# Up projection on unnormalised rows: the inverse root applied when the accumulators are evicted

## The chip, the cores and the metric

The kernel runs on one core of a Trainium2 chip. The metric is the device time of one execution in microseconds (us); the kernel before has a median of 2216.98 us over three runs (2213.57 to 2222.62).

## The reference, cut to what matters

One layer of a trunk is computed for 384 tokens (128 of a prompt, 256 of a sample), all in float32. The part around the change is the end of the mixer and the start of the feed-forward block:

```python
    x = x + g1 * y                      # y = mixer output @ w_out, D = 2048
    h2 = rmsnorm(x, lp['n2']) * (1.0 + sc2) + sh2
    x = x + g2 * conv_ffn(h2, lp['w_up'], lp['ffn_conv_w'], lp['ffn_conv_b'], lp['w_down'])

def conv_ffn(h, w_up, dw_w, dw_b, w_down):
    u, gv = jnp.split(h @ w_up, 2, axis=-1)      # 2 x 5632 columns
    u = depthwise_conv(u, dw_w, dw_b)            # 3 taps along the tokens
    return (jax.nn.silu(u) * gv) @ w_down
```

`rmsnorm` divides each token's row by the root of its mean square. The scales and shifts `sc2`, `sh2` belong to a channel and to the prompt or the sample.

## The kernel before, in words

**Split products.** Every large matmul is done in the reduced-precision float32 type three times: each operand is split into a high part and a low part, and high times high, high times low and low times high are added up in the same accumulator (`three`, lines 760 to 764). A weight part of 128x1024 is split by ScalarE (`hi`, line 1293) and VectorE (`lo`, line 1622); four such parts are held at a time, so `hi(n)` waits until TensorE has used part n-4. Parts are numbered through all stages. The `w_out` stage has parts P_OUT to P_OUT+31, eight to each of four blocks of 512 output columns; the `w_up` stage has P_UP to P_UP+175, four to each of 44 blocks of 256 columns (22 pairs: a block of `u`, then its block of `gv`). I write part P_UP+4 as "up part 4", and so on.

**Weights from memory.** SyncE alone issues the weight loads (line 501), 1 MB each, which is two parts, into a ring of four pieces. A load waits until the piece it overwrites has been split. In the first pair of the up stage something stands between the loads:

```python
            for i in range(DFF // BLK):
                load_block(P_UP + 2 * PARTS * i, a["w_up"][0], BLK * i, BLK)
                if i == 0:
                    sp.wait_ge(s_oc, 3 * N_OUT)
                    sp.dma_start(X_dram.rearrange("t p c -> p t c"), x2).then_inc(s_xs, 16)
                load_block(P_UP + 2 * PARTS * i + PARTS, a["w_up"][0], DFF + BLK * i, BLK)
```

So the loads of up parts 4 to 7 are issued after the residual of the last output block is finished (`s_oc` is 12) and after the store of `x2` (3 MB) to `x_mid`.

**The output projection.** TensorE runs the blocks j = 0 to 3 (`out_part`). VectorE adds each block, gated, to `x2` (`residual`, lines 2006 and 2007: six operations of 128x512). ScalarE squares it with a running sum (`squares`, line 1498).

**The transition.** When all four blocks are in `x2`, VectorE reduces the squares, GpSimd raises to the power -1/2 (line 652), VectorE scales `x2` by the root (line 2030), TensorE transposes it (`turn2`, lines 1213 and 1220: 48 transposes of 128x128), ScalarE and VectorE apply scale and shift (lines 1517 and 2036), and ScalarE and VectorE split the result (lines 1523 and 2041) into `h_split`, high and low, 16 rows of 384 words each (one for each 128 channels). `h_split` held the output projection's moving data before. Half of the transposes are placed ahead of the first up part and the rest behind up parts 0 and 1.

**The up projection.** The weights are stationary, 128x128; 384 columns of `h_split` stream past them. It has 22 x 2 x 2 x 16 x 3 = 4224 matmuls. Each pair's `u` accumulators are copied by ScalarE to `up2` (lines 1543, 1544), convolved by VectorE (2076 to 2078), passed through SiLU by ScalarE (1554) and multiplied with `gv` from its accumulators by VectorE (2086, 2087) into `act`. The down projection then splits `act` (lines 1564 and 2111) as its stationary operand.

Engines run their instructions strictly in the program's order. The printed functions below stand as they are in the kernel before.

Of the kernel before, what the change touches and what calls it, by code (L numbers as in the profile page):

```python
# [29 lines left out]
CHUNK = 64  # L30
DFF = 11 * D // 4
# [3 lines left out]
BT = 4  # L35
# [187 lines left out]
def build(nc, a, out):  # L223
    ctx = ExitStack()
    with ctx:
# [31 lines left out]
        NA = 52900 - C_END - 4 * P - 2 * KT - 192 - 2 * KT - 64 - 11 - RING * PIECE - 2 * SPLITS * PART - 2 * KT * TOK - 2400  # L257
# [5 lines left out]
        with ExitStack() as early:  # L263
            wsp = sb("w_split", 2 * SPLITS * PART, F32R, early)
            hsp = sb("h_split", 2 * KT * TOK, F32R, early)
            asp = sb("a_split", 2400, F32R, early)
        wmix = sb("w_mix", 2 * SPLITS * PART)
        hf = sb("h_f32", 2 * KT * TOK)
        ubuf = sb("u_buf", 2400)
        hh = hsp[:, 0:KT * TOK].rearrange("p (k n) -> p k n", k=KT)  # L270
        hl = hsp[:, KT * TOK:].rearrange("p (k n) -> p k n", k=KT)
# [42 lines left out]
        assert o <= 2400  # L314
# [47 lines left out]
        late = [(ubuf, HW * i) for i in range(2400 // HW)]  # L362
# [16 lines left out]
        xn2, o = carve(arena, o, 3, D)  # L379
        assert o <= NA  # L380
        ytmp, _ = carve(ubuf, 0, 2, OUT_W)
        mtmp, o = carve(ubuf, 0, 4, TOK)
        ssq2, o = carve(ubuf, o, 3, N_OUT)
        assert o <= 2400
# [7 lines left out]
        assert o <= 2400  # L392
# [14 lines left out]
        s_const, s_x, s_vrow, s_lnrow = sem("s_const"), sem("s_x"), sem("s_vrow"), sem("s_lnrow")  # L407
# [13 lines left out]
        s_rpl, s_rdp = sem("s_rpl"), sem("s_rdp")  # L421
# [22 lines left out]
        s_ssq2, s_xn2, s_xtp, s_xts, s_h2 = sem("s_ssq2"), sem("s_xn2"), sem("s_xtp"), sem("s_xts"), sem("s_h2")  # L444
# [24 lines left out]
        def used(eng, n):  # L469

            if n < P_DOWN:
                eng.wait_ge(s_blk, DONE.get(n, n + 1))
            else:
                eng.wait_ge(s_kd, n - P_DOWN + 1)

# [281 lines left out]
        def _(pe):  # L757
# [445 lines left out]

            for j in range(N_OUT):
                for p in range(0 if j else 3, OUT_PARTS):
                    out_part(j, p)

            def turn2(q):
                pe.wait_ge(s_xn2, q + 1)
                if q >= 2:  # L1210
                    pe.wait_ge(s_hmp, 4 * (q - 1))
                for k in range(4 * q, 4 * q + 4):
                    last = tr(ps[:, 6 + q % 2, toks(k % 4)], xn2[:, 0, toks(k)], ident)
                last.then_inc(s_xtp, 1)
                for j in range(2):
                    if q:
                        pe.wait_ge(s_hms, 4 * (q - 1) + 2 * j + 2)
                    for k in range(2):
                        for t in range(2):
                            last = tr(ps[:, 4 + j, P * (2 * k + t):P * (2 * k + t + 1)], xn2[:, 1 + t, toks(4 * q + 2 * j + k)], ident)  # L1220
                    last.then_inc(s_xts, 1)

            pe.wait_ge(s_oc, 3 * N_OUT)
            turn2(0)
            turn2(1)
            for i in range(DFF // BLK):
                for w in range(2):
                    if i >= 2:
                        pe.wait_ge(s_uc if w == 0 else s_uact, 2 * (i - 1))
                    for p in range(PARTS):  # L1230
                        n = P_UP + PARTS * (2 * i + w) + p
                        pe.wait_ge(s_lo, rank(n) + 1)
                        if i == 0 and w == 0:
                            pe.wait_ge(s_h2, KQ * (p + 1))
                        w_hi, w_lo = parts(n, KQ)
                        for s in range(2):
                            for k in range(KQ):
                                q = KQ * p + k
                                last = three(ps[:, 4 * (i % 2) + 2 * w + s, 0:TOK], w_hi[:, k, toks(s)], w_lo[:, k, toks(s)],
                                             hh[:, q, :], hl[:, q, :], start=(q == 0), stop=(q == KT - 1))  # L1240
# [37 lines left out]
        def _(ac):  # L1278
# [216 lines left out]
            def squares(j):  # L1495
                ac.wait_ge(s_oc, 3 * (j + 1))
                for t in range(3):
                    AC(xn2[:, t, OUT_W * j:OUT_W * j + OUT_W], x2[:, t, OUT_W * j:OUT_W * j + OUT_W], ACT.Square, accum_out=ssq2[:, t, j:j + 1]).then_inc(s_ssq2, 1)

            for n in range(P_OUT, P_UP):  # L1500
                if n >= P_OUT + 2 * OUT_PARTS and (n - P_OUT) % OUT_PARTS == OUT_PARTS // 2:
                    squares((n - P_OUT) // OUT_PARTS - 2)
                if n == P_OUT + 3:
                    ac.wait_ge(s_fy, 3 * GROUPS)
                if n > P_OUT + 2:
                    hi(n)
# [6 lines left out]
            def mod_p(k):  # L1513
                ac.wait_ge(s_xtp, k // 4 + 1)
                if k >= 4:
                    ac.wait_ge(s_h2, k - 3)
                AC(mtmp[:, k % 4, 0:P], ps[:, 6 + k // 4 % 2, toks(k % 4)], ACT.Identity, scale=scol[:, k, 0:1],
                   bias=modcol[:, 3 * KT + k, 0:1]).then_inc(s_hmp, 1)

            def h2_hi(k):  # L1520
                ac.wait_ge(s_hms, k + 1)
                ac.wait_ge(s_hmp, k + 1)
                AC(hh[:, k, :], mtmp[:, k % 4], ACT.Copy).then_inc(s_hh2, 1)

            for k in range(KT + 1):
                if k < KT:
                    mod_p(k)
                if k:
                    h2_hi(k - 1)
# [674 lines left out]
```

## Time and profile before

| what | value |
|---|---|
| median of 3 runs | 2216.98 us (2213.57 to 2222.62) |
| the profiled execution | 2212.79 us, of which the trace spans 2211.0 us |
| TensorE busy | 2078.0 us, 94% of the span |
| VectorE busy | 1058.3 us, 48% |
| ScalarE busy | 746.3 us, 34% |
| granted TensorE clock, mean | 0.978 of full speed |
| mean memory traffic | 155 GB/s |

All times below count from the start of the trace's span. "Busy" of TensorE is modelled for its pipelined matmuls, so where matmuls follow each other the distance from start to start is the cost of one. The output projection ends near 1068 us, the up projection near 1826 us.

### The profile page before, as it was taken

Reading aid. Unit: us, or ns where it says so; the run is one execution under the profiler, and the core shown is the slowest. Engines: PE = TensorE matmul, PEld = TensorE weight load, DVE = VectorE, ACT = ScalarE, POOL = GpSimd, SP = SyncE. Lnnn points to the kernel's source line nnn. Section 1 sums busy time; section 2 is a strip of 40 time slices with the busy share of each in tenths; the row PEclk is TensorE's granted clock in tenths of the full one; section 3 lists DMA queues with packets and bytes.
Section 4 is the critical chain, followed back from the end, with each engine's and each line's share of the span. In section 5 each row is a group of like instructions: output and inputs, shape, how many; then the busy total and the mean of one; then the engine's idle time right before and its main releaser. Section 6 shows DMA issues by size and latency. Waiting matters only on the chain.

```text
span 2211.0 us, 43887 instructions
## 1 busy us (share of the span) xinstructions
PE 2078.0 (94%) x19367; PEld 1818.5 (82%) x19367; DVE 1058.3 (48%) x1833; ACT 746.3 (34%) x1230; POOL 154.7 (7%) x248
## 2 busy tenths in 40 slices
PE   4899999999878888899799999999999999999997
PEld 2688888777557777788699999999999998887886
DVE  1432225555557777653644444444444444445444
ACT  2331222222455444423433223323323333333433
POOL 1000000000324434200000000000000000000000
PEclk8899999999899999999899999999999999999999
DMA  9888778776410010173343343343343436443341
GB/s 387 323 280 293 284 251 285 264 280 215 104 31 9 11 23 13 61 266 115 133 134 125 123 134 121 127 133 118 130 133 116 133 128 234 133 131 101 131 133 58
DMA packets 195999, 343.01 MB, mean 155 GB/s; under 512 B 14253, under 2 KB 137827, under 8 KB 193696
## 3 DMA queue, kind: packets, MB, share of 16 engines
q1 hardware_dynamic: 194416, 335.14, 44.4%
q0 software_dynamic: 1392, 5.05, 0.8%
q8 instruction: 153, 2.51, 0.5%
q14 instruction: 38, 0.31, 0.0%
HBM read 332.62 MB, written 10.31 MB: 155 GB/s over the span
## 4 chain that ended last, share of the span: by engine, by line
PE 85%; DVE 8%; DMA 2%; issue 2%; ACT 2%; POOL 1%; DVEq 0%; POOLq 0%; ACTq 0%
PE ps L762 25%; PE ps L764 24%; PE ps L763 24%; PE ps L796 4%; DMA ring<-in_w_mod_dram 1%; PE ps L1118 1%; PE ps L993 1%; PE ps L1001 1%; PE ps L995 1%; POOL w_mix L652 0%; PE ps L1011 0%; DVE h_split L1684 0%; PE ps L944 0%; PE ps L928 0%; PE ps L914 0%
## 5 line engine op out<-in xcount | busy, mean ns | idle before, releaser
L1622 DVE TENSOR_TENSOR w_split<-ring,w_split 128x1024 fp32r<-128x1024 f32 (+1 forms) x392 | 475.3, 1219 | 724.9 <-ACT w_split L1293 724.4
L1293 ACT ACTIVATE w_split<-ring 128x1024 fp32r<-128x1024 f32 (+1 forms) x392 | 406.8, 1051 | 827.0 <-PE ps L764 561.3
L762 PE MATMUL ps<-h_split,w_split 128*128 128x384 f32 x1776 | 599.9, 338 | 10.7 <-DVE w_split L1622 6.4
L764 PE MATMUL ps<-h_split,w_split 128*128 128x384 f32 x1776 | 596.5, 336 | 0.0
L763 PE MATMUL ps<-h_split,w_split 128*128 128x384 f32 x1776 | 596.4, 336 | 0.0
L762 PEld LDWEIGHTS ps<-h_split,w_split 128*128 128x128 f32 x1776 | 335.6, 189 | 23.9 <-issue 16.1
L763 PEld LDWEIGHTS ps<-h_split,w_split 128*128 128x128 f32 x1776 | 335.5, 189 | 0.0
L764 PEld LDWEIGHTS ps<-h_split,w_split 128*128 128x128 f32 x1776 | 335.4, 189 | 0.0
L762 PE MATMUL ps<-w_split,h_split 128*128 128x512 f32 (+1 forms) x528 | 199.4, 378 | 1.1 <-DVE w_split L1622 1.1
L763 PE MATMUL ps<-w_split,h_split 128*128 128x512 f32 (+1 forms) x528 | 195.9, 371 | 0.0
L764 PE MATMUL ps<-w_split,h_split 128*128 128x512 f32 (+1 forms) x528 | 195.7, 371 | 0.0
L762 PE MATMUL ps<-w_split,a_split 128*128 128x512 f32 x348 | 136.6, 393 | 6.1 <-DVE h_f L2100 4.8
L764 PE MATMUL ps<-w_split,a_split 128*128 128x512 f32 x348 | 136.5, 392 | 0.0
L763 PE MATMUL ps<-w_split,a_split 128*128 128x512 f32 x348 | 136.2, 391 | 0.0
L762 PEld LDWEIGHTS ps<-w_split,h_split 128*128 128x128 f32 x528 | 99.6, 189 | 29.0 <-issue 8.3
L796 PE MATMUL ps<-ring,c 128*2 128x256 f32 x1536 | 104.6, 406 | 17.2 <-DMA ring<-in_w_mod_dram 14.4
L764 PEld LDWEIGHTS ps<-w_split,h_split 128*128 128x128 f32 x528 | 99.7, 189 | 17.1
L763 PEld LDWEIGHTS ps<-w_split,h_split 128*128 128x128 f32 x528 | 99.7, 189 | 16.1
L652 POOL TENSOR_TENSOR stat<-stat,expb 128x3 f32<-128x3 f32 (+1 forms) x6 | 5.7, 953 | 1297.3 <-DVE stat L2134 1126.7
L796 PEld LDWEIGHTS ps<-ring,c 128*2 128x2 f32 x1536 | 34.2, 87 | 71.0 <-issue 24.0
L762 PEld LDWEIGHTS ps<-w_split,a_split 128*128 128x128 f32 x348 | 65.6, 188 | 21.4 <-DVE h_f L2100 6.0
L1564 ACT ACTIVATE a_split<-arena 128x384 fp32r<-128x384 f32 x58 | 30.4, 526 | 152.9 <-PE ps L764 152.8
(368 smaller groups left out, 2505.5 us busy)
## 6 DMA issues: line engine op xcount, KB each, us to landing
ring<-in_w_mod_dram SPq DMA_DIRECT2D x96, 1024.0 KB, 8.2
ring<-in_w_up_dram SPq DMA_DIRECT2D x88, 1024.0 KB, 5.1
ring<-in_w_in_dram SPq DMA_DIRECT2D x46, 1024.0 KB, 5.6
ring<-in_w_down_dram SPq DMA_DIRECT2D x44, 1024.0 KB, 5.3
ring<-in_w_out_dram SPq DMA_DIRECT2D x16, 1024.0 KB, 5.6
arena<-in_x_sample_dram SPq DMA_DIRECT2D x4, 1024.0 KB, 15.0
x_mid<-arena SPq DMA_DIRECT2D x1, 3072.0 KB, 10.2
h_f<-x_mid SPq DMA_DIRECT2D x1, 3072.0 KB, 10.2
```

The lines of the kernel that those rows point to most:

```text
L652: nc.gpsimd.tensor_tensor(ap, ap, minus_half.broadcast_to(list(ap.shape)), ALU.pow).then_inc(done, 1)
L762: mm(o_, lh, rh, start=start, stop=False)
L763: mm(o_, lh, rl, start=False, stop=False)
L764: return mm(o_, ll, rh, start=False, stop=stop)
L796: last = mm(ps[32 * g:32 * g + 2, i % 2, 0:BLK], c2_t[:, 2 * q:2 * q + 2], w_raw[:, g, :], start=(q == 0), stop=(q == KT - 1))
L993: mm(ps[half(hp), 4 * z + c, at], Nm[z][half(c), h, :], TTm[z][half(c), h, :], start=True, stop=True)
L995: last = mm(ps[half(hp), 4 * z + c, at], TTm[z][half(c), h, :], ident[half(c), half(c)], start=True, stop=True)
L1001: last = mm(ps[half(c), 4 * z + hp, HD * i:HD * i + HD], XT[z][half(hp), c, 1, HD * i:HD * i + HD], XT[z][half(hp), c, 0, HD * i:HD * i + ...
L1118: last = mm(o_, bkT[z][half(hp), q, i, c], zrT[z][half(hp), i, :, c], start=True, stop=True)
L1293: AC(wh[k % SPLITS][:, 0:width(n)], arrived(n), ACT.Copy).then_inc(s_hi, 1)
L1564: AC(ah[i % 3], act[:, i % FT, :], ACT.Copy).then_inc(s_ah, 1)
L1622: V.tensor_tensor(wl[k % SPLITS][:, 0:w], arrived(n), wh[k % SPLITS][:, 0:w].bitcast(F32), ALU.subtract).then_inc(s_lo, 1)
```

## The change

- **No normalisation ahead of the transposes.** `x2` itself is transposed. The inverse root of each token is applied when the up accumulators are evicted: VectorE multiplies two accumulators at a time (`up_raw`, `act_raw`) with a row of roots `rrow`. That row is made by three small matmuls of a constant with diagonal matrices of the roots (`root_row`), placed behind up part 4.
- **The shift as two more columns.** `sh2` must not be multiplied by the root, so it is streamed as two extra columns of the moving operand (prompt and sample). Every up matmul has 386 columns (`UPC`), and the rows of the split operand are 388 words apart (`UPS`). The product of the shift is added at eviction, as a bias on ScalarE and in a combined operation on VectorE.
- **Transposes and splits inside the last output blocks.** `turn2(k)` now does one block of 128 channels (three transposes); k = 0 to 11 are placed ahead of the last two parts of output blocks 1 to 3. The splits `h2_hi` and `h2_lo` of k = 0 to 11 are placed among weight parts 30 to 34 (`H2_AT`), each waiting until the output projection has used what it overwrites (`y_free`). k = 12 to 15 need the last block's residual; their transposes stand in the middle of up part 2, and their scaling and splitting stand behind the splits of up parts 4 and 5 on both engines.
- **Squares spread.** `squares(2)` and `squares(3)` stand behind the splits of up parts 3 and 5; each square now waits for the one before it. The residuals of blocks 0 to 2 are placed earlier among the weight splits.
- SyncE's program is not changed.

```diff
+UPC = TOK + 2
+UPS = TOK + 4
...
             for j in range(N_OUT):
                 for p in range(0 if j else 3, OUT_PARTS):
+                    if j and p >= OUT_PARTS - 2:
+                        turn2(4 * (j - 1) + 2 * (p - OUT_PARTS + 2))
+                        turn2(4 * (j - 1) + 2 * (p - OUT_PARTS + 2) + 1)
                     out_part(j, p)
...
-                        if i == 0 and w == 0:
-                            pe.wait_ge(s_h2, KQ * (p + 1))
...
+                                if i == w == s == 0:
+                                    pe.wait_ge(s_h2, 9 if q < 8 else 14 if q < 12 else h2_count(q))
+                                last = three(ps[:, 4 * (i % 2) + 2 * w + s, 0:UPC], w_hi[:, k, toks(s)], w_lo[:, k, toks(s)],
+                                             h2h[:, q, 0:UPC], h2l[:, q, 0:UPC], start=(q == 0), stop=(q == KT - 1))
+                            if (i, w, p, s) == (0, 0, 2, 0):
+                                for k in range(12, KT):
+                                    turn2(k)
                         last.then_inc(s_blk, 1)
-                        if i == 0 and w == 0 and p < 2:
-                            turn2(p + 2)
+                        if (i, w, p) == (0, 1, 0):
+                            root_row()
...
+            shift_hi(1)
             squares(N_OUT - 2)
-            for p in range(PARTS):
-                hi(P_UP + p)
+            hi(P_UP + PARTS)
+            hi(P_UP + PARTS + 1)
             squares(N_OUT - 1)
+            scale_even(12)
+            h2_hi(12)
+            scale_even(14)
+            for k in range(13, KT):
+                h2_hi(k)
...
+            shift_lo(1)
             residual(N_OUT - 1)
+            lo(P_UP + PARTS)
+            lo(P_UP + PARTS + 1)
+            scale_odd(13)
+            h2_lo(12)
+            scale_odd(15)
+            for k in range(13, KT):
+                h2_lo(k)
 
             dv.wait_ge(s_ssq2, 3 * N_OUT)
...
+                    V.tensor_copy(shift_up, ps[:, b_:b_ + 2, TOK:UPC])
+                    V.tensor_tensor(up_raw, ps[:, b_:b_ + 2, 0:TOK], rrow.unsqueeze(1).to_broadcast([P, 2, TOK]), ALU.mult).then_inc(s_uraw, 1)
...
+                    V.tensor_copy(shift_act, ps[:, b_:b_ + 2, TOK:UPC])
+                    link(V.tensor_tensor(act_raw, ps[:, b_:b_ + 2, 0:TOK], rrow.unsqueeze(1).to_broadcast([P, 2, TOK]), ALU.mult))
```

## Rows read from the trace of the kernel before

**Rows 1.** Windows: length, busy time of PE, PEld, DVE, ACT, POOL (records), granted clock, DMA share, GB/s.
```profile
1068.50:1086.80 18.30, 4.92 (x25) 4.44 (x25) 15.15 (x31) 7.76 (x19) 0.85 (x1) 0.67 0.73 258
...
1088.00:1090.00 2.00, 2.00 (x8) 2.00 (x7) 1.76 (x4) 0.66 (x2) 0.00 (x0) 0.50 1.10 350
...
1200.00:1300.00 100.00, 100.00 (x578) 100.00 (x578) 42.29 (x55) 30.61 (x42) 0.00 (x0) 1.00 0.39 127
```

**Rows 2.** Timeline, all engines, end of the output projection to the first up matmul.
```profile
1068.18 0.39 PE L764 MATMUL ps<-w_split,h_split 128*128 128x512 f32 x1
1068.61 0.69 DVE L2006 TENSOR_TENSOR u_buf<-ps,arena 128x512 f32<-128x512 f32 x1 [1.41 <-PE ps L764]
1068.67 1.06 ACT L1293 ACTIVATE w_split<-ring 128x1024 fp32r<-128x1024 f32 x1 [2.73 <-PE ps L764]
...
1072.96 0.63 ACT L1498 ACTIVATE arena<-arena 128x512 f32<-128x512 f32 x1 [3.24 <-DVE arena L2007]
1072.97 1.22 DVE L1622 TENSOR_TENSOR w_split<-ring,w_split 128x1024 fp32r<-128x1024 f32 x1
...
1074.94 0.17 DVE L2024 TENSOR_REDUCE stat<-u_buf 128x3 f32<-128x12 f32 x1 [0.75 <-ACT arena L1498]
...
1086.80 0.66 PE L762 MATMUL ps<-h_split,w_split 128*128 128x384 f32 x1 [2.13 <-DVE h_split L2041]
```

**Rows 3.** Timeline of TensorE, first up parts.
```profile
1091.72 0.34 PE L762 MATMUL ps<-h_split,w_split 128*128 128x384 f32 x1
...
1093.29 0.60 PE L1213 MATMUL ps<-consts,arena 128*128 128x128 f32 x4
1093.72 1.04 PE L1220 MATMUL ps<-consts,arena 128*128 128x128 f32 x8
...
1102.13 0.41 PE L762 MATMUL ps<-h_split,w_split 128*128 128x384 f32 x1 [0.83 <-DVE h_split L2041]
```

**Rows 4.** Issues of the DMA view, windows at 1030 and 1073 us: KB, us to landing.
```profile
ring<-in_w_up_dram SPq DMA_DIRECT2D x1, 1024.0 KB, 5.2
...
x_mid<-arena SPq DMA_DIRECT2D x1, 3072.0 KB, 10.2
ring<-in_w_up_dram SPq DMA_DIRECT2D x1, 1024.0 KB, 13.8
```

**Rows 5.** Timeline, then waits, of SyncE's queue, 1000 to 1140 us.
```profile
1030.22 8.53 SPq L501 DMA_DIRECT2D ring<-in_w_up_dram  x2
1072.96 0.37 SPq L606 DMA_DIRECT2D x_mid<-arena  x1
1073.37 65.11 SPq L501 DMA_DIRECT2D ring<-in_w_up_dram  x9
...
SPq L606 <- DVE arena L2007: 34.2, 1, 34.2
```

**Rows 6.** Timeline of ScalarE after the splits of `h_split`.
```profile
1105.12 2.94 ACT L1293 ACTIVATE w_split<-ring 128x1024 fp32r<-128x1024 f32 x3
...
1111.93 0.38 ACT L1544 ACTIVATE u_buf<-ps 128x256 f32<-128x256 f32 x1
```

**Rows 7.** Timeline of TensorE at other widths of the moving operand.
```profile
1055.04 0.39 PE L763 MATMUL ps<-w_split,h_split 128*128 128x512 f32 x1
...
1055.72 0.39 PE L763 MATMUL ps<-w_split,h_split 128*128 128x512 f32 x1
...
544.79 0.28 PE L763 MATMUL ps<-w_split,h_split 128*128 128x256 f32 x1
...
545.15 0.28 PE L763 MATMUL ps<-w_split,h_split 128*128 128x256 f32 x1
...
563.00 1.17 PE L873 MATMUL ps<-u_buf,consts 128*128 128x399 f32 x3
564.01 0.82 PE L876 MATMUL ps<-consts,arena 128*128 128x128 f32 x6
```

**Rows 8.** Groups by line and shape, VectorE, 940 to 2211 us: busy us, mean ns.
```profile
L2041 DVE TENSOR_TENSOR h_split<-u_buf,h_split 128x384 fp32r<-128x384 f32 x16 | 8.8, 550 | 0.2 <-ACT h_split L1523 0.2
```

More of the change, by code:

```diff
@@ L361, in build @@
         assert o <= O_RKV, (o, O_RKV)
-        late = [(ubuf, HW * i) for i in range(2400 // HW)]
+        late = [(ubuf, HW * i) for i in range(2368 // HW)]
         late += [(arena, o + HW * i) for i in range((O_RKV - o) // HW)]
@@ L391, in build @@
         sg2, o = carve(ubuf, o, 2, TOK + 1)
-        assert o <= 2400
+        assert o <= 2368
         x3, o = carve(hf, 0, 3, D)
@@ L1202, in _, with turn2, root_row @@
             pe.wait_ge(s_cyh, 1)
+            def turn2(k):
+                pe.wait_ge(s_oc, 3 * (k // 4 + 1))
+                if 2 <= k < 14:
+                    pe.wait_ge(s_hms if k % 2 else s_hmp, k // 2)
+                for t in range(3):
+                    last = tr(ps[:, 6 + k % 2 if k < 14 else k - 10, toks(t)], x2[:, t, toks(k)], ident)
+                last.then_inc(s_xtp, 1)
             for j in range(N_OUT):
                 for p in range(0 if j else 3, OUT_PARTS):
+                    if j and p >= OUT_PARTS - 2:
+                        turn2(4 * (j - 1) + 2 * (p - OUT_PARTS + 2))
+                        turn2(4 * (j - 1) + 2 * (p - OUT_PARTS + 2) + 1)
                     out_part(j, p)
[L1208 to L1225, printed above, removed]
+            def root_row():
+                pe.wait_ge(s_rdiag, 1)
+                for t in range(3):
+                    last = mm(ps[:, 6, toks(t)], consts[:, C_MEAN:C_MEAN + P], rdiag[:, t, :], start=True, stop=True)
+                last.then_inc(s_rrow, 1)
             for i in range(DFF // BLK):
@@ L1497, in squares @@
                 for t in range(3):
[L1498 to L1503, printed above, removed]
-                    ac.wait_ge(s_fy, 3 * GROUPS)
-                if n > P_OUT + 2:
-                    hi(n)
+                    AC(junk_sq, x2[:, t, OUT_W * j:OUT_W * j + OUT_W], ACT.Square, accum_out=ssq2[:, t, j:j + 1]).then_inc(s_ssq2, 1)
@@ new lines, in shift_hi @@
+            def shift_hi(q):
+                ac.wait_ge(s_blk, y_free(8 * q + 7, 0))
+                AC(h2h[:, 8 * q:8 * q + 8, TOK:UPC], modcol[:, 3 * KT + 8 * q:3 * KT + 8 * q + 8, :], ACT.Copy).then_inc(s_hh2, 1)
+            for n in range(P_OUT + 3, P_UP + PARTS):
+                m = n - P_OUT
+                if m >= 2 * OUT_PARTS and m % OUT_PARTS == OUT_PARTS // 2:
+                    squares(m // OUT_PARTS - 2)
+                if m == 3:
+                    ac.wait_ge(s_fy, 3 * GROUPS)
+                if m >= 2 * OUT_PARTS and m % OUT_PARTS in (1, 2):
+                    scale_even(4 * (m // OUT_PARTS - 2) + 2 * (m % OUT_PARTS - 1))
+                hi(n)
+                for k in H2_AT.get(m, ()):
+                    h2_hi(k)
+                if m == OUT_PARTS * N_OUT + 1:
+                    shift_hi(0)
@@ L1520, in h2_hi @@
[L1520 to L1529, printed above, removed]
+            scale_even(12)
+            h2_hi(12)
+            scale_even(14)
+            for k in range(13, KT):
+                h2_hi(k)
             for b in range(2 * (DFF // BLK) + 1):
@@ L1532, in _ @@
                 if b < 2 * (DFF // BLK):
-                    for p in range(PARTS if b else 0):
+                    for p in range(2 if b == 1 else 0, PARTS if b else 0):
                         hi(P_UP + PARTS * b + p)
@@ L1999, in _, with residual @@
             dv.wait_ge(s_fc, 3 * GROUPS)
-            def residual(j):
+            def residual(j, tiles=range(3)):
                 used(dv, P_OUT + OUT_PARTS * (j + 1) - 1)
-                for t in range(3):
+                for t in tiles:
                     n = 3 * j + t
@@ L2061, in _ @@
                 if b < 2 * (DFF // BLK):
-                    for p in range(PARTS if b else 0):
+                    for p in range(2 if b == 1 else 0, PARTS if b else 0):
                         lo(P_UP + PARTS * b + p)
@@ L2084, in _ @@
                         dv.wait_ge(s_usg, f + 1)
[L2085 to L2087 removed]
+                        V.scalar_tensor_tensor(act[:, f, 0:P], act_raw[:, s, 0:P], shift_act[:, s, 0:1], sg2[:, s, 0:P], ALU.add, ALU.mult)
+                        V.scalar_tensor_tensor(act[:, f, P:TOK], act_raw[:, s, P:TOK], shift_act[:, s, 1:2], sg2[:, s, P + 1:TOK + 1], ALU.add, ALU.mult).then_inc(s_uact, 1)
             lo(P_DOWN + SPLITS - 1)
```

150 lines of the change are left out of this document (88 added, 62 removed).

## The prediction

> **What bounds the kernel now.** I read the page first, then windows, then timelines. In the up projection TensorE is without a gap at full clock while VectorE is busy 42% and ScalarE 31% of the time [rows 1]. So there only what TensorE does itself costs time. The place where it idles is the transition: in 18.30 us it works 4.92 us [rows 1], because residual, squares, root, scaling, transposes and splits follow one another [rows 2].
>
> Call T the end of the output projection. The last matmul starts at 1068.18 [rows 2], one lasts 0.227 us from start to start (three in 0.68 us [rows 7]), so T = 1068.41. I count up to the point where no loss follows: up part 2 starts at 1102.13 [rows 3], and from T to there 33.72 us pass. By then 48 of the up matmuls are done, at 173.3 ns each (577 starts to 100 us would be 173.3, the row has 578 [rows 1]), which is 8.32 us. **The transition loses 33.72 - 8.32 = 25.40 us.** This is all that the change can attack, and 0.5% of the time is 11.1 us, about what a measurement of this kernel can tell from no change.
>
> **Transposes and roots on TensorE.** Four transposes take 1093.72 - 1093.29 = 0.43 us [rows 3], 0.108 each. The 36 of k = 0 to 11 go into the output blocks, where TensorE is the bound: 3.9 us. They wait for nothing: their residuals are finished parts earlier, and the splits of weights that run ahead by four parts of 4.1 us give ScalarE and VectorE the room for the scaling. The 12 of k = 12 to 15 cost 1.3 us in up part 2. The three root matmuls are true float32 ones of 128 columns; the nearest row, 399 columns, takes (564.01 - 563.00)/3 = 0.337 us a record [rows 7], so at 128 columns, two records each, between 0.4 us (by columns, the whole being 6 x 0.108 = 0.65) and 2.0 us (6 x 0.337); I take 0.7, as by columns.
>
> **The start of the up projection.** Parts 0 and 1 need k = 0 to 7, whose splits are queued among weight parts 30 to 33 and are done some 5 us ahead of T. k = 8 to 11 stand behind weight part 34, which can be split when part 30 is used, 4.7 us before T. Four high and low splits at 0.55 us [rows 8] end near T + 1, and the shift's splits behind weight part 35 near T + 2.8; both are needed at T + 8.3. So TensorE starts at T, not at T + 18.4 (1086.80), and at full clock.
>
> TensorE then runs 48 matmuls (8.3 us), 12 of part 2 (2.1 us), 12 transposes (1.3 us; their `s_oc` of 12 comes at T + 7.1, below) and 12 more matmuls, and comes to k = 12 in part 3 at **T + 13.8**.
>
> **What k = 12 waits for.** This is the step that decides. On ScalarE `scale_even(12)` stands behind the splits of up parts 4 and 5, on VectorE `scale_odd(13)` and `h2_lo(12)` too. These weights are loaded only after the last residual, behind the 3 MB store; SyncE's program is unchanged. Before, SyncE sat 34.2 us on that wait [rows 5], issued the store at 1072.96 and the load 0.41 us later [rows 5]. That load took 13.8 us to land where an undisturbed one takes 5.2, since the store took 10.2 [rows 4]. It landed at 1087.2, hidden, because ScalarE wanted it only at 1105.12 [rows 6]. The change removes that cover. Step by step from T:
>
> - The high split of part 35 starts 0.26 after T and takes 1.06 [rows 2]; the low split takes 1.22 [rows 2]: T + 2.55. `shift_lo(1)`: 0.2, T + 2.75.
> - The residual's six operations take 1072.96 - 1068.61 = 4.35 [rows 2]: T + 7.1. (Before, it came first, at T + 4.55.)
> - Store issued, load 0.41 later, landed 13.8 after: **T + 21.3**.
> - ScalarE: two splits, 1.06 + 0.98 (three take 2.94 [rows 6]), T + 23.35. `squares(3)`: before 1.98 [rows 2], now each waits for the last; between 2.0 and 2.8, I take 2.4: T + 25.75. Scaling: 0.38 for the wider of its two evictions [rows 6], about 0.55 for both. High split about 0.5, by [rows 8]: T + 26.8.
> - VectorE's low split 0.55 and the semaphores: **T + 27.6**.
>
> TensorE idles 27.6 - 13.8 = **13.8 us**. Queued behind ScalarE's wait are the squares too, so the root comes at about T + 33; `root_row` is wanted after up part 4, at T + 39, so that is covered. k = 13 comes another 0.3 us late, then the rows keep pace.
>
> **The clock.** Before, after the idle transition, TensorE ran at 0.50, its level of 1.2 GHz, until 1091.72 [rows 1, 3]: 15 matmuls in 4.92 us where full clock takes 2.60, a cost of 2.3 us. After 13.8 us of idling I expect the same 2.3.
>
> **Sum of the transition after:** 3.9 + 1.3 + 0.7 + 13.8 + 0.3 + 2.3 = 22.3 us, where 25.4 stood: a gain of 3.1.
>
> **Two more columns.** At full clock 512 columns take 226.7 ns, 384 take 173.3, 256 take 120 (three in 0.36 us) [rows 7, 1]: columns at 2.4 GHz and a fixed 13.3 ns. Two columns add 0.83 ns; times 4224 is 3.5 us, all of it on the bound. No row shows this operand type at a width or a row distance that isn't a multiple of 128 words. From below the cost is 0 (if the fixed part hid it; three widths on one line speak against that). From above: columns counted in sixteens, 400, would be 6.7 ns each, 28.2 us. I take the line, because rows of 399 words read by plain float32 matmuls, starting at any word, take 0.337 us for 2 x 399 columns, which is 332.5 ns and 4 ns more [rows 7]: no rounding and no misalignment shows.
>
> The Trainium skill (SBUF — State Buffer, Specifications) says that SBUF has 16-byte lines and that crossing to a new one is penalised. Rows 388 words apart keep their phase to such lines, and 386 words touch 97 lines where 384 touch 96. By that rule 388 columns' time would be paid, as an estimate 7.0 us in place of 3.5. No run here shows it.
>
> **Evictions.** To a pair of blocks (33.3 us) VectorE gets `up_raw` and `act_raw`, 768 elements each, between 0.69 (512 elements) and 1.22 (1024) [rows 2], about 0.95, and two tiny copies: 2.3 us more, where it idles 19 of 33 us [rows 1]. The weight splits queued behind run three parts ahead, 12.5 us, which hides this and ScalarE's wait for `up_raw`. Cover gone, it would be 22 x 2.3 = 50 us, but it would need VectorE to double. Only the last pair shows: the down projection's second weight operand waits for `act`; 1.3 us more in that chain, most of it behind 4.1 us of matmuls. I take 0.2 (0 to 1.3).
>
> **Total:** -3.1 + 3.5 + 0.2 = **+0.6 us**. Against its own execution, 2212.8 becomes 2213.4; that execution lies 4.2 us under the median. On the median: 2216.98 + 0.6 = 2217.6, say 2218.
>
> **Rivals.**
>
> *The load is not in the way* (faster). Then the transition loses 3.9 + 1.3 + 0.7 and some 1.5 us (0 to 3) for k = 12 to 15, which ScalarE and VectorE could bring at about T + 13 to T + 16: 7.4 us. Gain 18.0, less 3.7: 14.3, so 2203. For it: all else is ready. Against it: the load can't be issued before the residual is done, at T + 7.1, and would have to land at once; even a plain 5.2 us [rows 4] leaves 13.8 - 8.6 = 5.2 us idle, a gain of about 8.0, which is still within 0.5%. Past 0.5% needs 11.7 us off. I may have misread ScalarE's order or the overlap of store and load.
>
> *Matmuls of 386 columns cost more than their columns* (slower). Each ns is 4.2 us. The balance without the width is -2.9, so over 0.5% slower begins at 14.0 us, 3.3 ns each, eight columns' worth. In sixteens: 2217.0 - 2.9 + 28.2 = 2242. Against it speaks the float32 row, for it that this type may be read in another manner.
>
> *Columns in fours* (the rule above, as a mechanism: 388 in place of 386): 1.67 ns x 4224 = 7.0 us, 2217.0 - 2.9 + 7.0 = 2221, no change that can be told.
>
> *The whole does nothing*, as the gap was covered: excluded, since TensorE's idle time is on the chain.
>
> **Chances.** Forecast (stall of 10 to 17 us) 0.68, its own range 2213 to 2223; fours 0.07; load not in the way 0.13; wide matmuls 0.12. Hence faster 0.13, same 0.75, slower 0.12. The range, 2202 to 2227, takes in the faster case and leaves out most of the wide one and some of the tails.
>
> **What the profile after would show.** Up matmuls 174.2 ns apart (574 starts in 100 us, not 578); a first up matmul right behind the output projection; ScalarE waiting for DMA at line 1293 until about 21 us after T, the landing still 13 to 14 us after issue; TensorE idle for some 14 us in the fourth up part, then the low clock for about 15 matmuls. I am wrong if that wait is below 5 us, or if up matmuls stand more than 176 ns apart.

## The result, and the profile after

The changed kernel has a median of **2231.23 us** (2225.86 to 2232.21, five runs), the kernel before 2216.62 us in as many. The ratio is **1.0055**, 95% interval 1.004 to 1.007: slower, by 0.4 to 0.7% (12.2 us by the ratio, 14.6 us by the medians), where +0.6 us was forecast, and outside the range of 2202 to 2227. The profiled execution took 2231.81 us, of which the trace spans 2229.6.

Stretches of the changed kernel, in the windows view (columns as in [rows 1]): the transition, the stall in it, the matmuls after the stall, and two stretches inside the up projection.
```profile
1078.11:1111.40 33.29, 20.93 (x107) 20.37 (x106) 13.68 (x29) 11.42 (x25) 0.85 (x1) 0.79 0.75 252
1092.39:1104.65 12.26, 0.00 (x1) 0.03 (x1) 3.72 (x6) 6.12 (x14) 0.00 (x0) 0.70 1.07 337
1105.00:1111.00 6.00, 6.00 (x20) 5.77 (x20) 3.65 (x13) 1.72 (x3) 0.85 (x1) 0.51 0.81 255
...
1200.00:1300.00 100.00, 100.00 (x568) 100.00 (x567) 47.80 (x65) 30.69 (x40) 0.00 (x0) 1.00 0.39 126
1300.00:1700.00 400.00, 400.00 (x2263) 400.00 (x2262) 194.13 (x263) 126.95 (x167) 0.00 (x0) 1.00 0.38 124
```

The same execution in the timeline, all engines; what answers to [rows 2, 3, 5 and 6]:
```profile
1077.88 0.39 PE L787 MATMUL ps<-w_split,h_split 128*128 128x512 f32 x1
1078.11 0.33 PE L785 MATMUL ps<-h_split,w_split 128*128 128x386 f32 x1
...
1085.03 0.37 SPq L629 DMA_DIRECT2D x_mid<-arena  x1
1085.44 47.00 SPq L524 DMA_DIRECT2D ring<-in_w_up_dram  x8
...
1088.69 1.48 PE L1232 MATMUL ps<-consts,arena 128*128 128x128 f32 x12
...
1091.95 0.33 PE L787 MATMUL ps<-h_split,w_split 128*128 128x386 f32 x1
...
1098.34 2.00 ACT L1320 ACTIVATE w_split<-ring 128x1024 fp32r<-128x1024 f32 x2 [16.68 <-DMA ring<-in_w_up_dram]
...
1103.32 0.52 ACT L1540 ACTIVATE h_split<-arena 128x384 fp32r<-128x384 f32 x1
1103.94 0.56 DVE L2058 TENSOR_TENSOR h_split<-arena,h_split 128x384 fp32r<-128x384 f32 x1 [1.43 <-ACT h_split L1540]
1104.65 0.66 PE L785 MATMUL ps<-h_split,w_split 128*128 128x386 f32 x1 [12.36 <-DVE h_split L2058]
1105.11 0.53 PE L786 MATMUL ps<-h_split,w_split 128*128 128x386 f32 x1
...
1110.34 0.53 PE L787 MATMUL ps<-h_split,w_split 128*128 128x386 f32 x1
...
1111.13 0.34 PE L787 MATMUL ps<-h_split,w_split 128*128 128x386 f32 x1
1111.31 0.34 PE L785 MATMUL ps<-h_split,w_split 128*128 128x386 f32 x1
...
1116.04 0.83 PE L1245 MATMUL ps<-consts 128*128 128x128 f32 x6
...
1117.58 0.95 DVE L2124 TENSOR_TENSOR consts<-ps,consts 128x768 f32<-128x768 f32 x1
...
1129.29 0.34 PE L787 MATMUL ps<-h_split,w_split 128*128 128x386 f32 x1
...
1842.45 0.35 PE L787 MATMUL ps<-h_split,w_split 128*128 128x386 f32 x1
1842.64 0.40 PE L785 MATMUL ps<-w_split,a_first 128*128 128x512 f32 x1
```

And its waits (us in total, times, longest), then its DMA issues (KB, us to landing):
```profile
ACT w_split L1320 <- DMA ring<-in_w_up_dram: 16.7, 1, 16.7
...
PE ps L785 <- DVE h_split L2058: 12.4, 1, 12.4
```
```profile
x_mid<-arena SPq DMA_DIRECT2D x1, 3072.0 KB, 10.2
ring<-in_w_up_dram SPq DMA_DIRECT2D x2, 1024.0 KB, 14.1
```

What the reader is to see:

- The transition went as written. The up projection starts 0.23 us behind the last output matmul, so T = 1078.11. ScalarE waits for the load until T + 20.2, and TensorE stands still for 12.4 us ahead of up part 3. The weights of that part were split by T + 2.6 and the last transposes ended at T + 12.1; what is missing is the scaling and splitting of k = 12, queued on ScalarE and VectorE behind the splits of the late weights.
- The up projection has another pitch (distance from start to start). 400 us hold 2263 records, one more than distances: 176.8 ns. From 1129.29 to 1842.45 lie 168 parts of 24 matmuls: 713.16 / 4032 = **176.87 ns**, where before it was 173.3 [rows 1]. The clock is 1.00 in both. VectorE is busy 48% and ScalarE 31%, TensorE 100%, so nobody else sets this pace.

3.54 ns times 4224 is 14.95 us, as much as the whole loss; what the other stages gain and lose nearly cancels. By stages, from the starts of matmuls in each profiled execution:

| stage, us | before | changed | difference | forecast |
|---|---|---|---|---|
| output projection | 121.51 | 125.55 | +4.0 | +3.9 |
| T to the end of up part 3 | 41.96 | 33.55 | -8.4 | -7.6 |
| up parts 4 to 7 | 16.64 | 17.63 | +1.0 | +0.8 |
| up parts 8 to 175 | 698.88 | 713.16 | +14.3 | +3.4 |
| down projection | 372.20 | 374.50 | +2.3 | +0.2 |
| all ahead of the output projection | | | +5.6 | 0 |

The forecasts are the prediction's terms put into their stages: -25.4 + 1.3 + 13.8 + 0.3 + 2.3 and 0.1 of width for 96 matmuls. I don't put the last line down to the change: the chunked mixer's stage took 306.0 us in this execution and 302.1 in one of a version of the same program whose up rows begin 3 words later (the last but one experiment), with 6.8 us of low clock at its end in the first and none in the second, and its start varied by 5 us between the executions profiled. The other lines add up to +13.2 us.

### The profile page after: what moved, and what is told of

Its sections match the earlier page's. It is cut to its first block, busy times and chain, and to the rows that moved or that the text cites. A ratio compares the mean times of both kernels' runs of the same rounds, so it can differ in the third digit from the quotient of the medians.

```text
span 2229.6 us, 44006 instructions
## 1 busy us (share of the span) xinstructions
PE 2096.3 (94%) x19373; PEld 1835.6 (82%) x19373; DVE 1102.2 (49%) x1915; ACT 757.0 (34%) x1232; POOL 154.8 (7%) x248
## 4 chain that ended last, share of the span: by engine, by line
PE 86%; DVE 7%; DMA 2%; issue 2%; ACT 2%; POOL 1%; DVEq 0%; POOLq 0%; SPq 0%; ACTq 0%
PE ps L785 25%; PE ps L786 24%; PE ps L787 24%; PE ps L819 4%; DMA ring<-in_w_mod_dram 1%; PE ps L1016 1%; PE ps L1024 1%; PE ps L1141 1%; PE ps L1018 1%; PE ps L1034 1%; DMA ring<-in_w_up_dram 1%; DVE h_split L1723 0%; PE ps L967 0%; PE ps L951 0%; PE ps L937 0%
## 5 line engine op out<-in xcount | busy, mean ns | idle before, releaser
L785 PE MATMUL ps<-h_split,w_split 128*128 128x386 f32 (+1 forms) x1776 | 606.3, 341 | 21.5 <-DVE h_split L2058 12.4
L787 PE MATMUL ps<-h_split,w_split 128*128 128x386 f32 (+1 forms) x1776 | 604.1, 340 | 0.0
L786 PE MATMUL ps<-h_split,w_split 128*128 128x386 f32 (+1 forms) x1776 | 602.2, 339 | 0.0
L819 PE MATMUL ps<-ring,c 128*2 128x256 f32 x1536 | 103.0, 402 | 16.6 <-DMA ring<-in_w_mod_dram 13.8
L2166 DVE TENSOR_TENSOR a_split<-arena,a_split 128x384 fp32r<-128x384 f32 x58 | 32.3, 558 | 104.1 <-ACT a_split L1603 104.1
## 6 DMA issues: line engine op xcount, KB each, us to landing
x_mid<-arena SPq DMA_DIRECT2D x1, 3072.0 KB, 10.2
```

What stands on the lines that cost most here:

```text
L785: mm(o_, lh, rh, start=start, stop=False)
L786: mm(o_, lh, rl, start=False, stop=False)
L787: return mm(o_, ll, rh, start=False, stop=stop)
L819: last = mm(ps[32 * g:32 * g + 2, i % 2, 0:BLK], c2_t[:, 2 * q:2 * q + 2], w_raw[:, g, :], start=(q == 0), stop=(q == KT - 1))
L2166: V.tensor_tensor(al[i % 3], act[:, i % FT, :], ah[i % 3].bitcast(F32), ALU.subtract).then_inc(s_al, 1)
```

## The experiments

Two theories at first. *Width*: the whole loss is the pitch, and the transition's gain is real. *Load*: the stall behind the store has eaten a gain that is there to be had. They don't exclude each other, so each was undone alone and with the other, and matmuls were measured by themselves.

**Matmuls alone.** A loop of high times high, high times low, low times high over 16 rows, 192 matmuls for each setting; the other engines idle.

> This kernel computes nothing of the reference: it fills its outputs with zeros and runs 27 sections of 192 matmuls each, in the three-product pattern of the up projection, with all other engines idle. Only the width of the moving operand, the distance of its rows and its first word differ. In the profile of the changed kernel an up matmul of 386 columns costs 176.9 ns from start to start and one of 384 columns 173.3 before, where columns at 2.4 GHz give 174.2. Theory W (width: a moving operand whose width is not a multiple of some granule costs more in TensorE itself): section b (386 columns, rows 388 apart) and d (386, rows 384 apart) both near 177 ns, c (384, rows 388 apart) 173.3. Theory R (row distance): b and c near 177, d 174.2, f (386, rows 400 apart) and h (rows 392 apart) nearer to 174.2. Theory C (contention: VectorE's added evictions or other traffic in the real kernel): all sections lie on columns / 2.4 + 13.3 ns, b at 174.2.

The kernel took 939.33 us at a clock of 1.00. Starts of the first matmul of four settings, in its timeline: 384 columns with rows 384 words apart, 386 with 388, 384 with 388, 386 with 384.
```profile
62.83 0.33 PE L97 MATMUL ps<-h_split,w_split 128*128 128x384 f32 x1
...
96.11 0.34 PE L113 MATMUL ps<-h_split,w_split 128*128 128x386 f32 x1
...
130.07 0.33 PE L129 MATMUL ps<-h_split,w_split 128*128 128x384 f32 x1
...
163.70 0.35 PE L145 MATMUL ps<-h_split,w_split 128*128 128x386 f32 x1
```

192 distances each: 33.28 us, 33.96 and 33.63, so 173.3, 176.9 and 175.2 ns; 386 columns with rows 384 apart take 175.7. Width and distance each cost something, so neither theory W nor theory R holds alone. The loss is there with VectorE, ScalarE and the DMA queues idle, which refutes every cause outside TensorE and the width and place of what it reads and writes. The pitches used here (ns; "excess" is over columns / 2.4 + 13.33):

| columns | rows apart | start word | pitch | excess |
|---|---|---|---|---|
| 384 | 384 | 0 | 173.33 | 0.0 |
| 386 | 388 | 0 | 176.84 | 2.7 |
| 384 | 388 | 0 | 175.15 | 1.8 |
| 386 | 384 | 0 | 175.70 | 1.5 |
| 388 | 388 | 0 | 177.21 | 2.2 |
| 386 | 400 | 0 | 177.16 | 3.0 |
| 392 | 392 | 0 | 178.53 | 1.9 |
| 448 | 448 | 0 | 202.65 | 2.7 |
| 512 | 512 | 0 | 226.82 | 0.2 |
| 256 | 256 | 0 | 119.96 | 0.0 |
| 384 | 384 | 1 | 178.98 | 5.6 |
| 384 | 384 | 2 | 173.42 | 0.1 |
| 384 | 384 | 4 | 175.55 | 2.2 |
| 382 | 384 | 0 | 173.32 | 0.8 |
| 380 | 384 | 0 | 171.12 | -0.5 |
| 376 | 384 | 0 | 173.30 | 3.3 |
| 368 | 384 | 0 | 166.68 | 0.0 |
| 510 | 512 | 0 | 226.67 | 0.8 |
| 258 | 260 | 0 | 119.98 | -0.8 |

The rival of sixteens is dead too: 386 and 400 columns differ by 5.1 ns (177.16 on rows of 400, 182.26 for 400 of 400). What the three widths of [rows 7, 1] have in common is that their rows lie a multiple of 128 words apart, so all begin alike. That alone does not put a width on the line, though. The starts of the sections with 382, 380, 376 and 368 columns, all with rows 384 words apart from word 0:
```profile
613.29 0.33 PE L353 MATMUL ps<-h_split,w_split 128*128 128x382 f32 x1
...
646.57 0.34 PE L369 MATMUL ps<-h_split,w_split 128*128 128x380 f32 x1
...
679.43 0.33 PE L385 MATMUL ps<-h_split,w_split 128*128 128x376 f32 x1
...
712.70 0.33 PE L401 MATMUL ps<-h_split,w_split 128*128 128x368 f32 x1
```
376 columns cost as much as 384 (33.27 us for 192) and more than 380 (32.86). So the line through 256, 384 and 512 is no rule for the widths between: two columns more cost 0.0 ns from 382 to 384, 0.15 from 510 to 512 and 2.4 from 384 to 386.

**The load ahead of the store**, in the changed kernel:
```diff
                 load_block(P_UP + 2 * PARTS * i, a["w_up"][0], BLK * i, BLK)
+                load_block(P_UP + 2 * PARTS * i + PARTS, a["w_up"][0], DFF + BLK * i, BLK)
                 if i == 0:
                     sp.wait_ge(s_oc, 3 * N_OUT)
                     sp.dma_start(X_dram.rearrange("t p c -> p t c"), x2).then_inc(s_xs, 16)
-                load_block(P_UP + 2 * PARTS * i + PARTS, a["w_up"][0], DFF + BLK * i, BLK)
```
For the other pairs (i > 0) the loads keep their order.

> The changed kernel with the loads of up parts 4 to 7 issued ahead of the wait for the last residual and of the store. Theory of the stall (12.4 us of idling and the low clock behind it come from that load): ScalarE no longer waits for DMA in the transition, k = 12 is ready at about 13 to 15 us after the output projection's end, the idle time falls to under 3 us, and the time by 10 to 14 us, to about 2218 us. Rival (the splits on VectorE and ScalarE would be late anyway): idle time stays over 8 us, gain under 5 us.

Measured: 2213.68 us (12 runs, kernel before 2216.32 in 23), ratio 0.9993, interval 0.9982 to 1.0004. Timeline, waits and windows of it:
```profile
1040.44 25.31 SPq L524 DMA_DIRECT2D ring<-in_w_up_dram  x4
1087.36 0.37 SPq L629 DMA_DIRECT2D x_mid<-arena  x1
...
1095.55 0.44 PE L784 MATMUL ps<-h_split,w_split 128*128 128x386 f32 x1 [0.25 <-DVE h_split L2057]
```
```profile
PE ps L784 <- DVE h_split L2057: 0.3, 1, 0.3
```
```profile
1080.30:1100.00 19.70, 19.45 (x114) 18.85 (x113) 13.99 (x29) 11.91 (x26) 0.85 (x1) 1.00 0.61 219
```
Four loads are now issued ahead of the store. The stall falls from 12.4 to 0.3 us, and the clock in the transition is 1.00 where it was 0.51 after the stall: without the idling there is no low clock. T to the end of up part 3 takes 18.76 us in place of 33.55, which is 14.8 us: 12.1 of the stall, and 2.7 of slow matmuls, so more than the 10 to 14 expected. The pitch stays at 176.87.

**384 columns**: the shift's product is left out, rows stay 388 words apart.
```diff
-... ps[:, 4 * (i % 2) + 2 * w + s, 0:UPC], ..., h2h[:, q, 0:UPC], h2l[:, q, 0:UPC], ...
+... ps[:, 4 * (i % 2) + 2 * w + s, 0:TOK], ..., h2h[:, q, 0:TOK], h2l[:, q, 0:TOK], ...
```


> The changed kernel with up matmuls of 384 columns; rows stay 388 words apart. It leaves out the shift's product, so that the second shift is not computed (the evictions add what lies in the accumulators' next two columns). Theory W (width): start to start 173.3 ns, 3.5 x 4224 = 15 us less, about 2216 us. Theory R (row distance): start to start stays near 177 ns and the time near 2231 us. Theory C (contention by the evictions): start to start falls by 0.8 ns alone, 3.5 us less, 2228 us.

Measured: 2221.16 us (12 runs), ratio 1.0022, interval 1.0012 to 1.0033; pitch 175.28, stall 12.5 us. Taking the two columns away gives back 1.6 ns of 3.54: between theory W's 3.5 and theory R's 0, and twice theory C's 0.8. The other 1.95 is still there with the old width:
```profile
1300.00:1700.00 400.00, 400.00 (x2284) 400.00 (x2283) 192.53 (x257) 126.96 (x167) 0.00 (x0) 1.00 0.39 126
```
What differs from the kernel before in these matmuls is then the rows' distance, and that `w_split` and `h_split` both begin 96 words lower; for the distance alone, matmuls by themselves had 175.15.

**Both**, the shift's product left out and the load ahead:

> The two edits before together: loads first, and 384 columns (the second shift's product left out). If stall and width are independent and are all that went wrong, the gains add: about 25 to 29 us under the changed kernel, 2203 us, 14 us under the kernel before. If it stays above 2212 us, something else in the change costs time that neither run shows.

Measured: 2205.67 us (6 runs), ratio 0.9955, interval 0.9940 to 0.9970; pitch 175.28, stall 0.3 us. The load was worth 17.6 us in the medians with 386 columns and 15.5 with 384: the two terms add up to within 2 us.

**Where the rows start.** Beginning the rows 16 bytes (4 words) later had cost 2.2 ns at 384 columns, so place was scanned, rows and stationary tiles apart.

> A kernel of TensorE matmuls alone, 192 to a section, high part, low part, high part as in the up projection, all other engines idle; nothing of the reference is computed. What is changed is where the moving rows and the stationary tiles start, in words of 4 bytes: 384 columns with rows 384 words apart, all rows at one start (0, 1, 2, 3, 4, 6, 8, 12, 16, 24, 32, 48, 64, 96); the same with the rows at 0 and the stationary tiles moved by 2, 4, 8, 32, 64; the same with both moved alike by 2, 4, 8, 64; 386 columns with rows 512 apart at starts 0, 2, 4, 8, 64; 386 columns with rows 388 apart at starts 2, 4, 8, and with the tiles moved by 64. Theory two streams (what counts is how the moving row and the tile that is loaded beside it lie to each other): moving the tiles by n changes the pitch as moving the rows by n does (rows at word 4 had 175.55 ns in the first kernel, against 173.33 at 0), and with both moved alike the pitch is back at 173.3. Theory moving row alone (what counts is where the row's first and last word lie in the memory's lines): moving the tiles changes nothing (173.3 for all five), both moved alike gives the price of the rows alone (175.5 at 4), and every start with the same remainder by 16 words has the same pitch. Theory width (two columns past 384 have a price of their own): 386 columns with rows 512 apart stay 2.5 to 3 ns above the line of columns/2.4 + 13.33 (174.16) at every start, 176.9; by the theory two streams one of the starts brings them to 174.2.

Starts of the first matmul of five settings, 384 columns and rows 384 words apart from words 0, 1, 2, 3, 4, and of the setting behind them:
```profile
63.16 0.33 PE L99 MATMUL ps<-h_split,w_split 128*128 128x384 f32 x1
...
96.44 0.33 PE L116 MATMUL ps<-h_split,w_split 128*128 128x384 f32 x1
...
130.80 0.34 PE L133 MATMUL ps<-h_split,w_split 128*128 128x384 f32 x1
...
164.08 0.33 PE L150 MATMUL ps<-h_split,w_split 128*128 128x384 f32 x1
...
197.36 0.33 PE L167 MATMUL ps<-h_split,w_split 128*128 128x384 f32 x1
...
231.06 0.34 PE L184 MATMUL ps<-h_split,w_split 128*128 128x384 f32 x1
```
33.28, 34.36, 33.28, 33.28 and 33.70 us for 192: 173.3, 179.0, 173.3, 173.3 and 175.5 ns. Words 8, 16 and 64 cost nothing, 6 costs 2.8 ns, 12 1.7, 24 3.3, 32 2.7, 48 3.3, 96 2.7. Neither theory of the mechanism holds whole. *The moving row alone* falls: with the rows at 0, tiles moved by 32 words give 175.99 ns, and for 386 columns with rows 512 apart tiles moved by 4 bring 176.6 down to 173.35. *The two streams' difference alone* falls as well: tiles moved by 4 with 384 columns cost nothing where rows moved by 4 cost 2.2, and both moved alike by 2 cost 3.2 ns where either alone costs nothing. The theory of width falls: 386 columns with rows 512 apart from word 2 take 173.34 ns, the two columns for nothing.

**Does this hold in the real kernel?** In the *kernel before* the split operand's rows were moved against the split weights, by 4 and by 32 words. The room (8 and 32 words) comes off the arena that lies ahead of `w_split`, so `w_split` itself lies that much lower. The main lines of the edit for 4 words:
```diff
-            hsp = sb("h_split", 2 * KT * TOK, F32R, early)
+            hsp = sb("h_split", 2 * KT * TOK + 8, F32R, early)
...
-        hh = hsp[:, 0:KT * TOK].rearrange("p (k n) -> p k n", k=KT)
-        hl = hsp[:, KT * TOK:].rearrange("p (k n) -> p k n", k=KT)
+        hh = hsp[:, 4:4 + KT * TOK].rearrange("p (k n) -> p k n", k=KT)
+        hl = hsp[:, 4 + KT * TOK:4 + 2 * KT * TOK].rearrange("p (k n) -> p k n", k=KT)
```


> The kernel before, with the split operand's rows, 384 words apart as they were, begun 4 words (16 bytes) later against the split weights; the same instructions in the same order, nothing is left out. If the price of the matmul kernels carries over (384 columns from word 4: 175.5 ns against 173.34): the pitch of the up projection's matmuls goes from 173.3 to 175.5, its last 168 parts take 698.9 + 4032 x 2.17 ns = 707.6 us, and the kernel is 8 to 10 us slower (2225), more if the output projection's 512 columns are hit too. If where the rows start costs only in a kernel of matmuls alone, or if it was width alone that cost in the changed kernel: 173.3 ns, 698.9 us, 2216 us.

> The kernel before with the split operand's rows begun 32 words (128 bytes) later against the split weights; nothing is left out. If the price of the matmul kernels carries over (384 columns from word 32: 175.99 ns): pitch 176.0, last 168 parts of up 698.9 + 4032 x 2.65 ns = 709.6 us, kernel 10 to 12 us slower (2227). If 16-byte lines were what counts, a start that is a multiple of 128 bytes costs nothing: 173.3 ns, 2216 us.

Measured: 2240.02 us (4 runs; before 2220.43 in 7), ratio 1.0092, interval 1.0074 to 1.0111; and 2239.46 us, ratio 1.0096, interval 1.0078 to 1.0113. The same stretch of each, 4 words first:
```profile
1300.00:1700.00 400.00, 400.00 (x2280) 400.00 (x2280) 165.48 (x212) 121.41 (x167) 0.00 (x0) 1.00 0.38 124
```
```profile
1300.00:1700.00 400.00, 400.00 (x2275) 400.00 (x2274) 165.61 (x215) 121.32 (x167) 0.00 (x0) 1.00 0.39 125
```
The last 168 parts took 707.84 and 709.63 us, so 175.56 and 176.00 ns; forecast from the matmul kernels were 707.6 and 709.6. The same instructions lose 20 us to where two tensors lie. That is twice what the up projection explains. Of the rest 6.4 us are in the down projection: making room moved `w_split`, which is the moving operand there, against the stationary `a_split` and `a_first`, and the pitch over 300 of its matmuls of 512 columns went from 229.0 to 233.3 ns. Another 3.0 to 3.5 us are in the output projection, where `h_split` is the stationary operand: its pitch went from 226.7 ns to 233.3 (4 words) and 232.4 (32 words).

**386 columns, other places**, since the change needs that width:

> TensorE matmuls alone again, 192 to a section, 386 columns throughout; nothing of the reference is computed. Rows 388 words apart from starts 0, 1, 3, 6, 12, 14, 16, 32, and with the stationary tiles moved by 2, 4, 6, 8; rows 448 words apart from 0, 2, 4, 6; 416 from 0, 2; 392 from 2, 4, 6; 400 from 2, 4; 390 from 0, 2; 384 from 2, 4; 396, 404 and 408 from 0; 512 with tiles moved by 2, both by 2, and rows from 6. Theory one place for all rows (386 columns cost nothing over 384, 173.34 ns, where every row keeps a good place to the tile, as with rows 512 apart from word 2 in the second kernel): only the distances that are multiples of 128 words reach 173.3 at some start (384 from word 2), all others, whose rows come through many places, stay at 175.5 to 178. Theory distance alone: each distance has one price, whatever the start; 388 stays at 176.3 to 176.9 for all its starts.

Starts of the sections from words 0, 1 and 3, rows 388 words apart, and of the one behind:
```profile
64.07 0.34 PE L99 MATMUL ps<-h_split,w_split 128*128 128x386 f32 x1
...
98.03 0.34 PE L116 MATMUL ps<-h_split,w_split 128*128 128x386 f32 x1
...
132.16 0.33 PE L133 MATMUL ps<-h_split,w_split 128*128 128x386 f32 x1
...
165.64 0.33 PE L150 MATMUL ps<-h_split,w_split 128*128 128x386 f32 x1
```
Rows 388 words apart gave 176.84, 177.78, 176.54 and **174.42 ns** from words 0, 1, 2 and 3 (word 2 in the kernel before this one). I had expected one price for each distance, or that only multiples of 128 words reach the line; both are wrong. 448 words apart gave 176.7, 178.1, 175.0 and 180.0 from words 0, 2, 4 and 6; 384 apart from word 2 173.7; 512 apart with rows and tiles at 2 171.13, 3 ns under the line.

> TensorE matmuls alone, 192 to a section, nothing of the reference is computed. 386 columns with rows 388 words apart from word 3 (174.42 ns in the kernel before this one, 176.84 from word 0) with the stationary tiles at 0, 1, 2, 3, 4, 5, 64; from words 7, 11 and 5; rows and tiles at 1 and 1, 2 and 2, 1 and 2, 2 and 3, 0 and 1, 0 and 3; 384 columns with rows 384 apart and some odd starts of rows and tiles; rows 388 and 390 apart from odd starts. Theory remainder by four (rows 388 apart walk through all places that are 4 words apart, so only the start's remainder by 4 counts): words 7 and 11 give the 174.4 of word 3, word 5 the 177.8 of word 1, and tiles moved by 4 or 64 change nothing, tiles moved by 1 to 3 do. Theory of the moving row alone: tiles change nothing at any shift.

Words 7 and 11 gave 174.30 and 174.14 with word 3 at 174.45, word 5 177.47 with word 1 at 177.8: by fours, as expected, as far as these five starts tell (words 4, 8, 12, 16 and 32 lie at 176.3 to 176.9, as word 0 does). Tiles moved by 64 left word 3 at 174.29, by 4 made it 175.22, so "tiles by 4 change nothing" missed by 0.8 ns. No rows 390 apart got under 176.7.

**The rows at word 3, in the kernel.** Rows of 386 columns, 388 words apart as they were:
```diff
+UP0 = 3
...
-        h2h = hsp[:, 0:KT * UPS].rearrange("p (k n) -> p k n", k=KT)
-        h2l = hsp[:, KT * UPS:].rearrange("p (k n) -> p k n", k=KT)
+        h2h = hsp[:, UP0:UP0 + KT * UPS].rearrange("p (k n) -> p k n", k=KT)
+        h2l = hsp[:, UP0 + KT * UPS:UP0 + 2 * KT * UPS].rearrange("p (k n) -> p k n", k=KT)
```
First in the changed kernel as it is:

> The changed kernel itself, the load still behind the store, with its rows of 386 columns begun 3 words later against the split weights; nothing is left out. Theory (the width term was mis-sized because of where the rows lie): pitch 174.3 as with the load first, the last 168 parts of up 702.8 us where the changed kernel had 713.16, the stall of 12.4 us as it was; 2231.2 - 10.8 = about 2220.5 us. That is the size that the prediction's line gave (174.2 ns), so it would land near the forecast of 2218. Rival (the pitch gained was tied to the load's new place, by traffic or by the clock): 176.9 ns and 2231.

Measured: 2217.54 us (10 runs; before 2217.54 in 13), ratio 1.0005, interval 0.9992 to 1.0019. Stretch and wait:
```profile
1300.00:1700.00 400.00, 400.00 (x2296) 400.00 (x2296) 194.97 (x263) 127.88 (x168) 0.00 (x0) 1.00 0.39 127
```
```profile
PE ps L786 <- DVE h_split L2059: 12.5, 1, 12.5
```
The pitch is 174.31 ns, the last 168 parts take 702.8 us, the stall is as it was. With its width at the size that the prediction gave it (174.2 ns), the change makes no difference, as forecast.

Then with the load ahead of the store:

> The kernel with the load ahead of the store, and its rows of 386 columns, 388 words apart as they were, begun 3 words later against the split weights; nothing is left out. If the price of the matmul kernels carries over (174.42 ns from word 3 against 176.84 from word 0): pitch 176.87 - 2.4 = 174.4 to 174.5, the last 168 parts of up 703.3 us where they were 713.16, and the kernel 10 us under the one with the load first: 2203 to 2205, the fastest of those that compute everything, 0.5% under before. If writing the rows at odd words slows ScalarE's and VectorE's copies and subtractions at the start of up, some of it comes back there (their rows were 0.66 us each). If the places matter only for rows 384 apart: 176.9 ns and 2214.

Measured: **2205.03 us** (6 runs; before 2216.51 in 11), ratio 0.9949, interval 0.9931 to 0.9966. Stretch:
```profile
1300.00:1700.00 400.00, 400.00 (x2297) 400.00 (x2296) 195.71 (x264) 127.25 (x167) 0.00 (x0) 1.00 0.39 127
```
This is the fastest version, under the kernel before and, by 26 us, under the changed one. T to the end of up part 3 takes 18.61 us as from word 0 (18.76), so writing rows at odd words cost ScalarE and VectorE nothing that shows there.

## Why the prediction was wrong

- **The step that failed is "Two more columns"**: "Two columns add 0.83 ns; times 4224 is 3.5 us", with the line taken because the float32 rows showed "no rounding and no misalignment". It measured 3.54 ns and 14.95 us, 11.5 us more, which takes the forecast from +0.6 to +12.1 us, past the 11.1 us that can be told. That the width is paid on the bound was right; that its price follows the line through three widths was not: the price depends on where the rows lie, and on the width in steps that are off the line. Begun 3 words later, the same rows cost 174.31 ns, and the change as a whole makes no difference that can be told (ratio 1.0005). 384 columns at the new distance alone cost 1.95 ns in the kernel and the two columns 1.6 more. Which property of the places sets the price stays open. Nor do these 11.5 us account for the medians to the last: the down projection lost 2.1 us more than forecast, the transition gained 1.0 more, and 1.4 of the 14.6 us lie ahead of the output projection or in the spread of the runs. The evidence was too narrow in two ways: the three widths on the line [rows 7, 1] were themselves multiples of 128, with rows as far apart, and the 399-column row was another operand type with one matmul at a time to compare. The text said that no row showed this type at such a distance, and then gave all that could lie in that gap a chance of 0.19.
- **The rival "matmuls of 386 columns cost more than their columns"** is what happened, at half its price: past its threshold of 3.3 ns each (3.54), far from the 6.7 of sixteens. The reason given (columns counted in larger units) was not the cause: 386 columns can cost 173.3.
- **"Columns in fours"**: 1.67 ns each was forecast, 3.54 came. Rows begun 2 words later cost nothing and rows begun 32 words later 2.7 ns. The Trainium skill (SBUF — State Buffer, Specifications) has 16-byte lines and a penalty for each crossing to a new one, which would have it the other way round, so the measurement decides against that rule here.
- **The transition** was right in its parts. First up matmul behind the last output one: yes. Landing at T + 21.3: T + 20.2, 12.9 after issue. Stall 13.8: 12.4. Low clock after it at 0.51: some 20 matmuls in place of 15, 2.7 us in place of 2.3. Transposes in the output blocks 3.9: the stage grew by 4.0. `root_row` 0.7 (0.4 to 2.0): 0.83. Transposes of part 2 1.3: 1.48, the last one's full length in it. Together the transition gained 4.1 us where 3.1 was forecast.
- **"The load is not in the way"** was forecast to be worth 14.3 us against before. As a claim on the changed kernel it was wrong (the load was in the way); made true by its order, it gave 14.8 us from T to part 3 and 17.6 in the medians. What is then lost between T and that point beside 96 matmuls is 18.76 - 16.98 = 1.8 us.
- **The evictions** cost VectorE what was said (0.95 us each, 2.5 us to a pair where 2.3 was forecast), hidden throughout the up projection. **The down projection** grew by 2.3 us, not 0.2: 0.68 ns a matmul over 1583 is 1.1 us, a term that the prediction hasn't. `w_split` has moved against `a_first` by 96 words and against `a_split` by 128, and 8 words of such a move cost 4.3 ns in the experiment above; that this is the cause here was not tested by itself. Another 0.8 is what it took beyond the kernel with the load ahead (373.66), where the low clock in the middle of the stage lasted 6.8 us in place of 10.2. The remaining 0.4 is within the forecast's 0 to 1.3.

## What to carry to other kernels

Where TensorE is the bound, treat the place of both its operands as a cost: a change of a row's width or distance, or an allocation that shifts a tensor, moved the pitch here by up to 7 ns, and over thousands of matmuls a few ns outweigh a saved transition. Measure the pitch (start to start, at full clock, in windows of a few hundred us) of the very shape, distance and start before pricing it from neighbours, and scan a handful of starts: word 3 in place of word 0 was worth 10.4 us here for a few lines. And when a serial chain is shortened, look at what was issued behind it: the load that the chain had hidden took 15 of the 19 us gained, until it went ahead of the store.

## What was not expected of the hardware

- For 128x128 stationary and 384 moving columns of this float32 type, rows 384 words apart, start words alone change the pitch: 173.3 ns with rows from words 0, 2, 3, 7, 8 and 16, 179.0 from word 1, 180.0 with rows at 2 and tiles at 4. Both the rows' and the tiles' places count, and they don't count by their difference alone. The rule behind it stays open.
- The pitch can lie under columns / 2.4 + 13.33: 171.13 ns for 386 columns, 512 words apart, rows and tiles at word 2, where the line gives 174.16. 376 columns lie 3.3 ns over it at the same place where 384 are on it. So the 13.3 ns are no fixed cost.
- The price carries over from kernel to kernel to within 0.15 ns: for 384 columns 175.51 and 175.99 ns alone, 175.56 and 176.00 in the real one, and for 386 columns from word 3 174.42 and 174.31, with VectorE, ScalarE and the DMA queues at work beside it.
